# Four feed-forward layers with two plain unit groups and nine block groups each, and a new order of the ScalarE splits

## The reference

```python
def swiglu_2(x, w_gate, w_up, w_down):
    return (jax.nn.silu(x @ w_gate) * (x @ w_up)) @ w_down
...
    for l in range(DEPTH_2):
        x = layer_norm(ALPHA * x + 0.5 * swiglu_2(x, ffn1_gate[l], ffn1_up[l], ffn1_down[l]), ln_g[l, 0], ln_b[l, 0])
...
        x = layer_norm(ALPHA * x + mix, ln_g[l, 1], ln_b[l, 1])
        x = layer_norm(ALPHA * x + 0.5 * swiglu_2(x, ffn2_gate[l], ffn2_up[l], ffn2_down[l]), ln_g[l, 2], ln_b[l, 2])
```

## Time and profile before

| | |
|---|---|
| median of 3 runs | 2851.29 us (2851.05 to 2851.48) |
| profiled execution, its own time | 2854.89 us |
| span of the profile | 2853.1 us |
| TensorE busy | 2799.4 us, 98% of the span |
| VectorE, ScalarE, GpSimd busy | 60%, 41%, 21% |
| mean granted TensorE clock | 0.998 of full speed |
| bytes read from HBM | 320.04 MB, 113 GB/s over the span |

### The profile page before, as it was taken

How to read it: one execution, slowest core, us unless ns; L and a number is a source line. 1 busy time by engine, 2 the same in 40 slices (tenths; PEclk the granted TensorE clock), 3 DMA queues, 4 the chain that set the end, 5 groups by cost and what they waited for, 6 DMA issues and landing times.

```text
span 2853.1 us, 42204 instructions
## 1 busy us (share of the span) xinstructions
PE 2799.4 (98%) x17509; PEld 2443.0 (86%) x17509; DVE 1700.3 (60%) x2357; ACT 1162.6 (41%) x1577; POOL 608.8 (21%) x657
## 2 busy tenths in 40 slices
PE   9999999899999999999999999999999999999999
PEld 8888887678888799988887999889998887799987
DVE  5544343554333488854647988448885465788843
ACT  5232244653223254433434543336443343454432
POOL 0114616201110221110234111112111013421110
PEclk9999999999999999999999999999999999999999
DMA  4222223122222367632212676326762221367622
GB/s 151 96 97 98 93 75 95 47 82 96 96 96 96 105 160 181 161 101 84 90 60 91 170 172 160 104 87 168 180 171 96 82 89 54 104 161 179 163 96 81
DMA packets 123726, 326.06 MB, mean 114 GB/s; under 512 B 17360, under 2 KB 17488, under 8 KB 123536
## 3 DMA queue, kind: packets, MB, share of 16 engines
q1 hardware_dynamic: 100496, 281.41, 30.1%
q0 software_dynamic: 23040, 41.95, 9.8%
HBM read 320.04 MB, written 2.10 MB: 113 GB/s over the span
## 4 chain that ended last, share of the span: by engine, by line
PE 75%; DVE 12%; issue 4%; ACT 4%; DMA 3%; POOL 0%; SPq 0%; DVEq 0%; ACTq 0%; POOLq 0%
PE bank L399 16%; PE bank L400 16%; PE bank L401 16%; PE bank L587 5%; PE bank L591 4%; PE bank L589 4%; DMA praw<-weight_pairs 3%; PE bank L536 2%; DVE plo L1649 1%; ACT phi L1032 1%; PE bank L465 1%; PE bank L469 1%; PE bank L466 1%; PE bank L416 1%; PE bank L422 1%
## 5 line engine op out<-in xcount | busy, mean ns | idle before, releaser
L1632 DVE TENSOR_TENSOR wlo<-wraw,whi 128x1024 fp32r<-128x1024 f32 x311 | 399.4, 1296 | 447.5 <-ACT whi L1013 447.4
L1013 ACT ACTIVATE whi<-wraw 128x1024 fp32r<-128x1024 f32 x319 | 332.6, 1055 | 482.4 <-DMA wraw<-weights 482.3
L399 PE MATMUL bank<-Ah,whi 128*128 128x512 f32 x1056 | 412.9, 391 | 0.0
L401 PE MATMUL bank<-Al,whi 128*128 128x512 f32 x1056 | 411.0, 389 | 0.0
L400 PE MATMUL bank<-Ah,wlo 128*128 128x512 f32 x1056 | 410.9, 389 | 0.0
L399 PE MATMUL bank<-H,whi 128*128 128x512 f32 x984 | 386.9, 393 | 5.1 <-DVE H L1755 2.2
L401 PE MATMUL bank<-H,whi 128*128 128x512 f32 x984 | 383.3, 389 | 0.0
L400 PE MATMUL bank<-H,wlo 128*128 128x512 f32 x984 | 383.0, 389 | 0.0
L587 PE MATMUL bank<-TF,plo 128*128 128x256 f32 x1280 | 363.1, 284 | 2.2 <-ACT cb L1136 1.8
L589 PE MATMUL bank<-TF,phi 128*128 128x256 f32 x1280 | 362.2, 283 | 0.0
L591 PE MATMUL bank<-TF,phi 128*128 128x256 f32 x1280 | 362.2, 283 | 0.0
(11 more groups left out here) (352 smaller groups left out, 5048.6 us busy)
## 6 DMA issues: line engine op xcount, KB each, us to landing
wraw<-weights SPq DMA_DIRECT2D x319, 512.0 KB, 3.5
praw<-weight_pairs SPq DMA_DIRECT2D x160, 384.0 KB, 4.7
praw<-weight_pairs SPq DMA_DIRECT2D x160, 256.0 KB, 3.8
praw<-weight_pairs POOLq DMA_DIRECT2D x160, 256.0 KB, 4.3
X<-x_t SPq DMA_DIRECT2D x8, 256.0 KB, 6.9
y_t<-X SPq DMA_DIRECT2D x8, 256.0 KB, 2.1
dist<-attention SPq DMA_DIRECT2D x4, 256.0 KB, 4.0
wraw<-weights SPq DMA_DIRECT2D x2, 256.0 KB, 4.1
```

The lines of the kernel that those rows point to most:

```text
L399: pe.matmul(b, sh, mh, start=start, stop=False)
L401: signal(pe.matmul(b, sh, ml, start=False, stop=stop), keys)
L1013: act.activation(whi[:, u % NS, :], wraw[:, u % NS, :], ACT.Copy).then_inc(*S.done("weights_hi", ("hi", u)))
L1632: dve.tensor_tensor(wlo[:, u % NS, :], wraw[:, u % NS, :], f32(whi[:, u % NS, :]), SUB).then_inc(*S.done("weights_lo", ("lo", u)))
```

## The change

Each FFN gets a second plain group (j = 2), and the block groups are those from j = 4 on, nine instead of ten. N_PAIRS goes from 40 to 36. Around that:

- The token forms, the loads of the first pairs and their splits now stand beside the second plain group instead of the first. `token_sums` waits for the last row of `X`. The first `load_pairs` stands in SyncE's list behind the load of the eighth unit, where it was behind the fourth.
- The products of column blocks 0 and 1 go to `Af` directly, and their splits are made by `split_a`.
- In the loop over pairs ScalarE's list has `sum_hi` ahead of `first_product` and, for k = 1 to 3, ahead of `raw_hi`; before, `raw_hi` came first.
- The three `phi` slots are used in another rotation.

```diff
@@ -39,9 +39,9 @@
 NCOLS = _at
 
 FFN_TILES = NF // 2 * 4 * KD
-FIRST_TILES = 4 * KD
+FIRST_TILES = 8 * KD
 PAIRED = ("a0", "b0", "a1", "b1")
-N_PAIRS = (NF // 2 - 1) * 4
+N_PAIRS = (NF // 2 - 2) * 4
 HALF = T // 2
 KEPT = 4
 OUT_TILES = NF * KD
...
@@ -358,7 +360,7 @@
 
         li, s = divmod(v, N_PAIRS)
         q = START[PAIRED[li]] // 16 % 2
-        return (2, q, 3, 1 - q)[s % 4], (2, q, 1 - q)[s % 3]
+        return (2, q, 3, 1 - q)[s % 4], (q, 1 - q, 2)[s % 3]
 
     def row_done(st, k):
 
@@ -565,7 +567,7 @@
 
         def pair_group(st, j):
 
-            v0 = PAIRED.index(st) * N_PAIRS + (j - 2) * 2
+            v0 = PAIRED.index(st) * N_PAIRS + (j - 4) * 2
             use = (st, j)
             half = [slice(0, HALF), slice(HALF, T)]
             for k in range(4):
...
@@ -599,7 +601,8 @@
         def ffn(st, rms, idle):
             if st in PAIRED:
                 gemm_group((st, 0), st, (), None, idle)
-                for j in range(2, NF, 2):
+                gemm_group((st, 2), None)
+                for j in range(4, NF, 2):
                     pair_group(st, j)
                 return
             for j in range(0, NF, 2):
@@ -1017,10 +1020,10 @@
             s = v % N_PAIRS
             u0 = START[PAIRED[v // N_PAIRS]] // 8
             act.wait_ge(pair_in[raw], 16 * pair_landings(v))
-            if s == 0:
+            if s < 2:
+                act.wait_ge(*S.at(("unit", u0 + 2 * s + 5)))
+            elif s == 2:
                 act.wait_ge(*S.at(row_done(PAIRED[v // N_PAIRS], KD - 1)))
-            elif s < 3:
-                act.wait_ge(*S.at(("unit", u0 + 2 * s - 1)))
             else:
                 act.wait_ge(*S.at(("pair unit", v - 3)))
             act.activation(phi[hi_slot][:, 0:6, :], praw[raw][:, 2:8, :], ACT.Copy).then_inc(
@@ -1122,44 +1125,47 @@
             p = START[st]
             u0 = p // 8
             v0 = PAIRED.index(st) * N_PAIRS
-            for k in range(KD):
-                hi_to(p + 4 * k + 3, u0 + 3)
-            token_hi(st, 0)
-            raw_hi(v0)
-            token_hi(st, 1)
-            sum_hi(v0)
+            for j in (0, 2):
+                for k in range(KD):
+                    hi_to(p + 16 * j + 4 * k + 3, u0 + 7)
+                if j:
+                    for i in range(3):
+                        token_hi(st, i)
+                    raw_hi(v0)
+                    sum_hi(v0)
+                    token_hi(st, 3)
+                act.wait_ge(*S.at(("full", (st, j))))
+                for i in range(2):
+                    act.wait_ge(*S.at(("product", st, i) if j else tmp_free + (i,)))
+                    act.activation(tmp[i], bank(((st, j), i))[:, :], ACT.Silu).then_inc(
+                        *S.done("silu", ("silu", st, j + i), empties=[((st, j), i)]))
+                if not j:
+                    for key in arena_free:
+                        act.wait_ge(*S.at(key))
+                    for i in range(2):
+                        split_a(st, i)
             raw_hi(v0 + 1)
             sum_hi(v0 + 1)
-            act.wait_ge(*S.at(("full", (st, 0))))
-            for i in range(2):
-                act.wait_ge(*S.at(tmp_free + (i,)))
-                act.activation(tmp[i], bank(((st, 0), i))[:, :], ACT.Silu).then_inc(
-                    *S.done("silu", ("silu", st, i), empties=[((st, 0), i)]))
             raw_hi(v0 + 2)
-            token_hi(st, 2)
-            for key in arena_free:
-                act.wait_ge(*S.at(key))
-            for i in range(2):
-                act.wait_ge(*S.at(("product", st, i)))
-                act.activation(Ah[:, i, :], tmp[2 + i], ACT.Copy).then_inc(*S.done("moving_hi", ("Ah", st, i)))
-            token_hi(st, 3)
-            for j in range(2, NF, 2):
+            for j in range(4, NF, 2):
                 for k in range(4):
-                    s = 2 * (j - 2) + k
-                    if 0 < s < N_PAIRS - 2:
+                    s = 2 * (j - 4) + k
+                    if k == 0 and 0 < s < N_PAIRS - 2:
                         raw_hi(v0 + s + 2)
-                    if k == 3 and j < NF - 2:
-                        first_product(st, j)
-                    if k == 0 and j > 2:
+                    if k == 0 and j > 4:
                         silu_pair(st, j - 2)
                     if 0 < s < N_PAIRS - 1:
                         sum_hi(v0 + s + 1)
+                    if k == 3 and j < NF - 2:
+                        first_product(st, j)
+                    if k and s < N_PAIRS - 2:
+                        raw_hi(v0 + s + 2)
                     if s >= N_PAIRS - 2:
-                        hi(u0 + 4 + s - N_PAIRS + 2)
-                    if j == 2:
+                        hi(u0 + 8 + s - N_PAIRS + 2)
+                    if j == 4:
                         scale_rows(st, 2 * k)
                         scale_rows(st, 2 * k + 1)
-                    if j == 4 and k == 2:
+                    if j == 6 and k == 2:
                         for i in range(2, KEPT):
                             split_a(st, i)
             first_product(st, NF - 2)
@@ -1659,44 +1665,44 @@
             p = START[st]
             u0 = p // 8
             v0 = PAIRED.index(st) * N_PAIRS
-            for k in range(KD):
-                lo_to(p + 4 * k + 3, u0 + 3)
-            more_sums(v0)
-            token_lo(st, 0)
-            pair_lo(v0)
-            more_sums(v0 + 1)
-            sum_lo(v0)
-            token_lo(st, 1)
+            for j in (0, 2):
+                for k in range(KD):
+                    lo_to(p + 16 * j + 4 * k + 3, u0 + 7)
+                if j:
+                    for i in range(3):
+                        token_lo(st, i)
+                    more_sums(v0)
+                    pair_lo(v0)
+                    sum_lo(v0)
+                    token_lo(st, 3)
+                    more_sums(v0 + 1)
+                else:
+                    for key in arena_free:
+                        dve.wait_ge(*S.at(key))
+                dve.wait_ge(*S.at(("full", (st, j))))
+                for i in range(2):
+                    dve.wait_ge(*S.at(("silu", st, j + i)))
+                    dve.tensor_tensor(Af[:, j + i, :], bank(((st, j), 2 + i))[:, :], tmp[i], MUL).then_inc(
+                        *S.done("gates", ("product", st, j + i), empties=[((st, j), 2 + i)]))
+                if not j:
+                    for i in range(2):
+                        split_a(st, i)
             pair_lo(v0 + 1)
-            dve.wait_ge(*S.at(("full", (st, 0))))
-            for i in range(2):
-                dve.wait_ge(*S.at(("silu", st, i)))
-                dve.tensor_tensor(tmp[2 + i], bank(((st, 0), 2 + i))[:, :], tmp[i], MUL).then_inc(
-                    *S.done("gates", ("product", st, i), empties=[((st, 0), 2 + i)]))
             sum_lo(v0 + 1)
-            token_lo(st, 2)
-            for key in arena_free:
-                dve.wait_ge(*S.at(key))
-            for i in range(2):
-                dve.wait_ge(*S.at(("Ah", st, i)))
-                dve.tensor_tensor(Al[:, i, :], tmp[2 + i], f32(Ah[:, i, :]), SUB).then_inc(
-                    *S.done("moving_lo", ("Al", st, i)))
-            for j in range(2, NF, 2):
+            for j in range(4, NF, 2):
                 for k in range(4):
-                    s = 2 * (j - 2) + k
+                    s = 2 * (j - 4) + k
                     if 0 < s < N_PAIRS - 1:
                         more_sums(v0 + s + 1)
                         pair_lo(v0 + s + 1)
                         sum_lo(v0 + s + 1)
                     if s >= N_PAIRS - 2:
-                        lo(u0 + 4 + s - N_PAIRS + 2)
+                        lo(u0 + 8 + s - N_PAIRS + 2)
                     if k == 3:
                         blocks(st, j)
-                    if s == 1:
-                        token_lo(st, 3)
-                    if k == 1 and j > 2:
+                    if k == 1 and j > 4:
                         product(st, j - 2)
-                    if j == 4 and k == 2:
+                    if j == 6 and k == 2:
                         for i in range(2, KEPT):
                             split_a(st, i)
 
@@ -2445,8 +2451,7 @@
         def token_sums(st, k):
 
             a, b = slice(0, HALF), slice(HALF, T)
-            pool.wait_ge(*S.at(row_done(st, 2 * k)))
-            pool.wait_ge(*S.at(row_done(st, 2 * k + 1)))
+            pool.wait_ge(*S.at(row_done(st, KD - 1)))
             pool.tensor_tensor(Tf[:, 2, k, :], X[:, 2 * k, b], X[:, 2 * k + 1, b], SUB).then_inc(
                 *S.done("pool_pairs", ("T third", st, k)))
             pool.tensor_tensor(Tf[:, 0, k, :], X[:, 2 * k, a], X[:, 2 * k, b], SUB)
@@ -2463,8 +2468,8 @@
             token_sums(st, 0)
             token_sums(st, 1)
             token_sums(st, 2)
+            token_sums(st, 3)
             add_pairs(v0 + 1)
-            token_sums(st, 3)
             add_pairs(v0 + 2)
             for s in range(3, N_PAIRS):
                 add_pairs(v0 + s)
...
@@ -2658,7 +2663,7 @@
```

(14 more changed lines are left out.)

6 lines of the change are left out of this document (4 added, 2 removed).

## The result

The changed kernel takes 2833.7 us (median of 6 runs, 2832.07 to 2835.68), the one before 2851.37 us (6 runs). The ratio is 0.9939, with a 95% interval of 0.9926 to 0.9952: 17.7 us or 0.6% faster, against 15.3 us forecast. The profiled execution has a span of 2833.9 us, 19.2 less than before.

The account below looks back on a forecast made before the run. TensorE, busy 98% of the span, was taken as the bound, with small waits mostly between block groups. Terms +6.4, -23.4, +3.7 and -2.0 sum to -15.3 us: 2836.0 us against the median, range 2828 to 2848.

Parts of the forecast that it names:

- Dearer groups: A plain group replaces a block group in each FFN: 21.76 against 20.16 us, +6.4 us over four.
- `sum_hi` first: At passages between block groups, `sum_hi` runs beside `pair_lo`, so `blocks` starts earlier and nearly all loss goes: -23.4 us.
- The floor of -1.89: Earliest start of `blocks`, in us relative to the group's start, set by product 3 of the last pair; no loss there.
- the sign that the prediction named for rival C: VectorE's `more_sums` waiting for landings in most groups.
- rival C: Adding DMAs' landings become the limit between block groups: 0.4 us left in 32 passages, 12.8 instead of 2.0; 2847 us, chance 0.11.
- Start of the pairs: After the second plain group: pair 1 late by 2.4 us per FFN (+9.6), old first-pair losses gone (-5.9): +3.7 us.
- the 1 to 4 us named as a sign: In each FFN the step from pair 0 to 1 after the plain group is this much longer than 5.04 us.
- Rival B: GpSimd's token sums blocked beside VectorE take 3 us more, first pairs much later: +12 us, 2848 us; chance 0.11.
- Quiet first plain group: Token sums no longer run beside VectorE's `Hl` subtractions in the first plain group: -2.0 us, bounds 0 to -3.3.
- Rival D: `raw_hi` behind a late `sum_hi` delays `pair_lo` in every pair: slower, 2872 us at 0.25 us a pair; chance 0.08.

Follow-up runs that it names:

- e1: Kernel before with one edit: ScalarE's `sum_hi` ahead of `first_product` and, for k = 1 to 3, of `raw_hi`; one plain group kept. 2833.33 us, ratio 0.9941.
- e2: Changed kernel with ScalarE's old order put back (`raw_hi`, `first_product`, `sum_hi`), two plain groups kept. 2850.14 us, ratio 1.0001 to the kernel before.
- e4: Changed kernel with GpSimd's four token sums ahead of the adding DMA of pair 0. 2827.94 us, ratio 0.9921 to the kernel before.
- e5: Changed kernel with token sums ahead of the adding DMAs, each sum waiting only for its own two rows of `X`. 2827.08 us, ratio 0.9917.
- e9: Kernel before with the new ScalarE order, one plain group, and GpSimd's first token sum ahead of pair 0's adding DMA. 2830.62 us, ratio 0.9927.
- e3: Changed kernel with `first_product` alone put back ahead of `sum_hi`; `raw_hi` stays behind both. 2846.04 us, ratio 0.9984 to the kernel before.

## Why the prediction was right

The working forecast -15.3 us against the profiled span, and the mechanism that it named is the one that the runs show. Its terms, measured in the changed kernel's trace (the table above):

1. *Dearer groups*, +6.4: not separable from the pace; the pace of 21.76 and 5.04 us holds in both traces.
2. *`sum_hi` first*, -23.4: measured -22.1 (25.4 to 3.2). The floor of -1.89 was met in 27 passages. Late landings left 3.2 us, where 2.0 had been counted. VectorE now waits for landings in `more_sums` 23 times (24.4 us), 3 times before; at 16 of the 32 passages it does, so the sign that the prediction named for rival C was half met, and the time was not. Rival C's mechanism is there, at a quarter of the size that was feared (0.1 us a passage, not 0.4). e1 and e2 show that the order of ScalarE's list, this term, is the whole gain: with it alone the time is that of the change, and without it there is no gain.
3. *Start of the pairs*, +3.7: measured +2.5 (6.5 to 9.0). The chain came out link by link in a0: 4.19 us to the first add (4.7 taken), 16.5 from add to add (15.4), 5.2 until seen (5.3), and pair 1 at 1031.1 where the working, with t0 at 1001.65, gives 1030.9. Only its split was wrong. I had pair 0 on time; its `pair_lo`, behind the sums too, was late, which cost 0.6 to 1.1 us in each FFN (3.8 in all), and pair 1 lost 1.3 instead of 2.4 us on average, since pair 0 had already taken part of it. e4 shows the cause: without the add ahead of the sums both losses go. In a1 pair 1 lost 0.54 us, less than the 1 to 4 us named as a sign. Rival B (the sums blocked for 3 us more) did not come: from add to add it was 1.1 us more.
4. *Quiet first plain group*, -2.0, bounds 0 and -3.3: measured -4.5 (5.0 to 0.4, unrounded). This term was mis-sized, beyond its bound. I had summed only the waits that the timeline prints; the restart of TensorE after each, and small gaps without a printed wait, are nearly as much again (5.0 us of loss for 2.8 us of printed waits). The reason given, the token sums as such, is too broad: the long subtractions stand where a sum comes right behind an adding DMA (e5 and e9).

That makes -17.8 us in the four FFNs. Terms 2 and 3 missed by 1.3 us one way and 1.2 the other, so that they cancel is luck; the rest of the miss is term 4. The other 1.4 us of the 19.2 lie in stretches that the change doesn't touch: a0 starts at 979.80 instead of 981.96 us, and the mixers between are 0.8 us longer. This is taken as the scatter of one execution, which no run separates; the medians moved by 17.7 us.

Rival D (`raw_hi` too late behind `sum_hi`) did not come: no step from pair 1 to 2, or from 2 to 3, lost anything that shows.

## What to carry to other kernels

On an engine that runs in order, sort the instructions at a busy place by when their inputs are ready, not by when they seem to belong. A 0.6 us copy that waits for the slow engine must not stand ahead of one whose input is there; here that copy's place alone was worth 12.3 us, 0.4% (e3), and with `raw_hi` behind as well 0.6%. When an engine that looks idle on average (41% busy) feeds one that is short of time for 5 us in every 20, look at its list around those 5 us. And a large change that carries a small one is best taken apart: the second plain group, the larger part of this diff, was worth nothing by itself (ratio 1.0001). With the adding DMAs moved behind the sums as well, the kernel is another 6 us faster (e4); how much of that needs the second plain group is not settled: with one plain group only a part of that move was tried, the first sum ahead of the add, and it gave 2830.62 us (e9).
